# Moving the adaLN tiles, bias tables, two norm weights and the sink logits from SyncE's queue to GpSimd's, with a ring of three

## The reference

```python
# first block, D = 2048
mod = silu(c) @ w_ada + b_ada                  # w_ada is 2048 x 12288
sh1, sc1, ga1, sh2, sc2, ga2 = split(mod, 6)
h = modulate(rms_norm(x, g_norm1), sh1, sc1)
qa, ka, va, oa, gates, qb, kb, vb = split(h @ w_in)
h_a = mlstm_bidirectional(...)                 # 4 heads, then a norm times g_head_a * sigmoid(oa)
h_b = neighborhood_attention(qb, kb, vb, rpb)  # 8 heads, bias from the table rpb
x = x + ga1 * (concat([h_a, h_b]) @ w_out)
h = modulate(rms_norm(x, g_norm2), sh2, sc2)
x = x + ga2 * conv_glu(h, w_up, conv_w, conv_b, w_down)    # 2 x 5632 wide
x = rms_norm(x, g_final)
# second block
q..., ga, gb = split(rms_norm(x, norm_mix_g) @ w_in_2)
ya = sliding_window_attention(..., sink_logits) @ w_branch_a
yb = stick_breaking_attention(...) @ w_branch_b
x = x + (sigmoid(ga) * ya + sigmoid(gb) * yb) @ w_out_2
x = x + swiglu(rms_norm(x, norm_ffn_g), w_ffn_in, w_ffn_down)
return rms_norm(x, norm_final_g)
```

## Time and profile before

| | |
|---|---|
| times of three runs | 2805.21, 2807.12, 2807.06 us |
| median | 2807.06 us |
| the profiled execution, its time | 2805.28 us |
| the profiled execution, its span | 2803.5 us |
| mean granted TensorE clock in it | 0.993 of full |
| PE busy | 2632.0 us, 94% |
| DVE busy | 1647.8 us, 59% |
| ACT busy | 1203.2 us, 43% |
| POOL busy | 132.6 us, 5% |

### The profile page before, as it was taken

The page is one execution under the profiler, slowest core; times in us unless marked ns, Lnnn a source line. Parts: engine busy times, 40 slices in busy tenths (PEclk is TensorE's granted clock), DMA queues, the critical chain, the costliest instruction groups (busy, mean ns, idle before and its releaser), DMA issues.

```text
span 2803.5 us, 33726 instructions
## 1 busy us (share of the span) xinstructions
PE 2632.0 (94%) x11966; PEld 2153.8 (77%) x11966; DVE 1647.8 (59%) x1822; ACT 1203.2 (43%) x1516; POOL 132.6 (5%) x129
## 2 busy tenths in 40 slices
PE   0699998989999999999989999999999999999998
PEld 0577886778878788788878877778788888888886
DVE  8887674767767665644454465555555444454444
ACT  1143344434434343444444454554454454544443
POOL 2000003010000000000010030101000000000000
PEclk9999999999999999999999999999999999999999
DMA  9798776676767665555566644346566666666664
GB/s 397 275 339 276 251 263 168 206 237 197 245 202 240 194 194 165 187 189 192 167 203 191 191 121 143 100 140 219 162 185 188 192 188 188 188 189 191 194 193 147
DMA packets 273259, 567.38 MB, mean 202 GB/s; under 512 B 23956, under 2 KB 24300, under 8 KB 272652
## 3 DMA queue, kind: packets, MB, share of 16 engines
q1 hardware_dynamic: 272528, 565.78, 63.2%
q0 software_dynamic: 208, 0.18, 0.0%
q10 hardware_dynamic: 428, 0.14, 0.0%
HBM read 563.94 MB, written 2.10 MB: 202 GB/s over the span
## 4 chain that ended last, share of the span: by engine, by line
PE 82%; DVE 6%; DMA 5%; issue 3%; ACT 2%; SPq 1%; DVEq 0%; POOL 0%; POOLq 0%; ACTq 0%
PE gp L1127 25%; PE gp L1129 25%; PE gp L1128 25%; DMA raw<-in_w_in_dram 2%; DVE ada_sum L1622 2%; DMA ada_ring<-in_w_ada_dram 2%; DVE w_lo L1519 1%; ACT w_hi L685 1%; DMA proj<-in_w_ada_dram 1%; PE tp L1354 1%; PE tp L1396 1%; PE tp L1172 1%; PE tp L1163 0%; PE tp L1262 0%; DVE ff L1880 0%
## 5 line engine op out<-in xcount | busy, mean ns | idle before, releaser
L1519 DVE TENSOR_TENSOR w_lo<-raw,w_hi 128x1024 fp32r<-128x1024 f32 x872 | 1068.4, 1229 | 903.2 <-ACT w_hi L685 898.3
L685 ACT CAST w_hi<-raw 128x1024 fp32r<-128x1024 f32 x872 | 910.9, 1051 | 1114.8 <-PE gp L1129 896.1
L1127 PE MATMUL gp<-w_hi,h_hi 128*128 128x512 f32 x2656 | 1051.0, 396 | 33.7 <-DVE w_lo L1519 30.0
L1128 PE MATMUL gp<-w_lo,h_hi 128*128 128x512 f32 x2656 | 1036.2, 390 | 0.0
L1129 PE MATMUL gp<-w_hi,h_lo 128*128 128x512 f32 x2656 | 1036.1, 390 | 0.0
L1127 PEld LDWEIGHTS gp<-w_hi,h_hi 128*128 128x128 f32 x2656 | 499.6, 188 | 152.7 <-DVE w_lo L1519 40.9
L1129 PEld LDWEIGHTS gp<-w_hi,h_lo 128*128 128x128 f32 x2656 | 499.4, 188 | 106.1
L1128 PEld LDWEIGHTS gp<-w_lo,h_hi 128*128 128x128 f32 x2656 | 499.8, 188 | 100.7 <-issue 0.2
L1127 PE MATMUL gp<-w_hi,a_hi 128*128 128x512 f32 x704 | 274.7, 390 | 0.0
L1129 PE MATMUL gp<-w_hi,a_lo 128*128 128x512 f32 x704 | 273.9, 389 | 0.0
L1128 PE MATMUL gp<-w_lo,a_hi 128*128 128x512 f32 x704 | 273.9, 389 | 0.0
(11 more groups left out here) (264 smaller groups left out, 1436.0 us busy)
## 6 DMA issues: line engine op xcount, KB each, us to landing
raw<-in_w_in_dram SPq DMA_DIRECT2D x248, 512.0 KB, 4.4
raw<-in_w_up_dram SPq DMA_DIRECT2D x176, 512.0 KB, 4.3
raw<-in_w_ffn_in_dram SPq DMA_DIRECT2D x176, 512.0 KB, 4.2
ada_ring<-in_w_ada_dram SPq DMA_DIRECT2D x128, 512.0 KB, 4.6
raw<-in_w_down_dram SPq DMA_DIRECT2D x88, 512.0 KB, 3.7
raw<-in_w_ffn_down_dram SPq DMA_DIRECT2D x88, 512.0 KB, 4.6
proj<-in_w_ada_dram SPq DMA_DIRECT2D x64, 512.0 KB, 7.5
raw<-in_w_out_dram SPq DMA_DIRECT2D x64, 512.0 KB, 4.6
```

The source lines that it names most:

```text
L685: nc.scalar.copy(w_hi[:, s], raw[:, s]).then_inc(hi_ready, 1)
L1127: mm(o, hi[:, kt0 + kt, ps], w_hi[:, s, k, :], start=n == 0, stop=False)
L1128: mm(o, hi[:, kt0 + kt, ps], w_lo[:, s, k, :], start=False, stop=False)
L1519: V.tensor_tensor(w_lo[:, s], raw[:, s], w_hi[:, s].bitcast(F32), ALU.subtract).then_inc(lo_ready, 1)
```

## The change

All later adaLN tiles, the bias tables, g_final, the sink logits and norm_final_g_2 are issued by GpSimd, in one written-out order between its other work. The ring of adaLN tiles has three slots (AR = 3; the last 32 tiles, from PART3 on, use only two of them). SyncE issues x, the first 64 tiles, the blocks of weights and the output. GpSimd's first later tile stands behind the clearing of the sum buffer at L538 of the changed kernel. In `g_in_o` DVE now sums a tile at each odd block of both chunks, where it summed one at each of the first four. A few small buffers take the place of an unused one, so that the third slot fits.

```diff
+AR = 3
...
-        ada_ring = sb("ada_ring", [P, 2, ADA_W], scope=s1)
+        ada_ring = sb("ada_ring", [P, AR, ADA_W], scope=s1)
...
+        def ada_slot(a):
+            return (a - PART2) % AR if a < PART3 else (a - PART3) % 2
...
@@ SyncE
-            def ada(a, slot, k, col):
-                if not isinstance(a, int) or a >= PART2 + 2:
-                    sp.wait_ge(ada_summed, a - 1)
-                sp.dma_start(ada_ring[:, slot, :], w_ada[bass.ds(k * P, P), bass.ds(col, ADA_W)]
-                             ).then_inc(ada_landed[slot], 16)
...
-            def bias(n):
-                if n < 4:
-                    sp.wait_ge(ml_s, HA)
-                else:
-                    sp.wait_ge(na_s, n - 3)
...
-            stream(g_in_a, ada_in(0), g_in_b)
-            stream(g_in_b, ada_in(g_in_a.chunks), g_in_o)
-            stream(g_in_o, biases, g_out, unrolled=True)
-            stream(g_out, ada_out, g_up)
-            stream(g_up, None, g_down, early=ada_up)
-            stream(g_down, None, g_in2a)
-            sp.wait_ge(drained[1], g_down.chunk0 + g_down.chunks)
-            sp.dma_start(gate2[:, :], ... g_final ...)
-            sp.wait_ge(x_final, 2 * (g_out.chunks + g_down.chunks))
-            sp.dma_start(sink[:, :], ... sink_logits_2 ...)
...
+            for g, nxt in zip(gemms, gemms[1:]):
+                stream(g, nxt)
@@ GpSimd
+            def ada(a, k, col):
+                if a >= PART3 + 2:
+                    pool.wait_ge(ada_summed, a - 1)
+                elif a >= PART3:
+                    pool.wait_ge(ada_summed, PART3)
+                elif a >= PART2 + AR:
+                    pool.wait_ge(ada_summed, a - AR + 1)
+                s = ada_slot(a)
+                pool.dma_start(ada_ring[:, s, :], w_ada[k * P:(k + 1) * P, col:col + ADA_W]
+                               ).then_inc(ada_landed[s], 16)
...
+            for k in range(K1 - 1):
+                ada_cols(k)
+            for n in range(4):
+                bias(n)
+            ada_cols(K1 - 1)
+            for n in range(3):
+                ada_gate(n)
+            for n in range(4):
+                window(n)
+            ada_gate(3)
+            bias(4)
+            ada_gate(4)
+            bias(5)
+            window(4)
...
             pool.wait_ge(na_s, HB)
             link(nc.gpsimd.memset(gate2[:, :], 0.0))
             pool.dma_start(gate2[0:1, :], b_ada[0:1, 5 * D:6 * D]).then_inc(acc_bias[2], 16)
+            ada_mod(0, range(4))
+            ada_mod(1, range(4))
+            ada_mod(2, range(3))
+            add_x(g_out, xt1, 0)
...
+            for c_ in range(g_down.chunks):
+                add_x(g_down, ff, c_)
+            pool.wait_ge(drained[1], g_down.chunk0 + g_down.chunks)
+            pool.dma_start(gate2[:, :], ... g_final ...)
+            pool.dma_start(sink[:, :], ... sink_logits_2 ...)
@@ VectorE, in g_in_o
-                if j < 4:
-                    n = 4 * e + j
-                    dve.wait_ge(ada_landed[n % 2], 16 * (3 * K1 + n // 2 + 1))
+                if j % 2:
+                    n = (e * g_in_o.nb + j) // 2
+                    dve.wait_ge(ada_landed[ada_slot(PART2B + n)], ada_count(PART2B + n))
```

167 lines of the change are left out of this document (80 added, 87 removed).

## The result

The changed kernel takes 2785.23 us (median of four runs, 2783.74 to 2786.3), the kernel before 2807.09 (2805.21 to 2808.13): a ratio of 0.992, with an interval of 0.9908 to 0.9932. The forecast was 2785.0. The sum came out right. But two of its terms, A and D, come from the third slot and not from the queue, and C only in part from the queue; that is what most of this part is about.

What follows compares the result with a forecast made beforehand. The prediction took the kernel to be bound by its matmuls on PE. Terms 5.0 + 1.3 + 13.4 + 1.8 + 1.5 - 0.7 = 22.3 us off 2805.28 gave 2783.0, as a median 2784.8, stated as 2785; range 2777 to 2798.

Steps and rivals of the forecast that it cites:

- A: First projection: SyncE no longer stands in adaLN issues that wait for DVE's sums, so weights run ahead; gain 5.0 us.
- D: `g_out`: weights loaded ahead let DVE's delay beside POOL's addition fall into the ring's slack; gain 1.8 us.
- C: Second projection to `g_in_o`: weights no longer stand behind bias transfers and adaLN tiles on SyncE; gain 13.4 us.
- With SyncE free of them the weights run as far ahead as their ring lets them: First projection: freed of four adaLN issues taking 7.61 us, SyncE issues weights earlier; 5.0 of 5.6 us taken.
- B: Gates of the mLSTM: gate-logit copies no longer stand behind a DVE sum waiting for its tile; gain 1.3 us.
- E: Into the second block: weights come earlier without g_final and the sink logits on SyncE; gain 1.5 us.
- F: Start of `g_up`: 32 tiles still use two slots, and slower landing from POOL lengthens DVE's wait; loss 0.7 us.
- Landings of 9 to 11 us: Rival: POOL's tiles land that late, costing gains in `g_in_a`; 2791 to 2798 us, chance 0.14.
- The slower rival: `g_in_a`: POOL writes descriptors only in DVE's gaps, so landings stretch to 13 to 15 us; 2829 to 2853, chance 0.09.
- The rival of the bias tables: Before `g_in_o`: eight slow bias issues on POOL hold up the last set of six tiles; 2794 us, chance 0.10.

## Why the prediction was right, and where it wasn't

**A, 5.0 forecast, 4.9 to 5.1 measured, and for half of the reason.** The step "With SyncE free of them the weights run as far ahead as their ring lets them" named the queue as the cause. The path was right, since ACT waited 69.6 us for weights from 120 to 240 us of the kernel before. But with SyncE free and two slots the gain is gone (-0.8), and with everything on SyncE and three slots it is whole (5.2). What limited the stretch was the round trip of a slot: wait for the sum, issue, landing, next sum. By the prediction's own formula two slots leave 2 x 2.70 - 1.28 = 4.1 us for issue and landing where tiles stand in adjacent blocks, and they took 0.34 + 4.3 from SyncE and 0.53 + 4.3 from GpSimd; three slots leave 6.8, and the changed kernel took 0.53 + 5.9. SyncE's 7.61 us were that round trip, seen from the engine that stood in it. The prediction did say that the third slot was the cover on which the move to GpSimd rests, and the run with the ring of two bears that out; it failed to ask what the slot does by itself.

**B, 1.3 forecast, 1.0 to 1.1 in its stretch.** DVE's wait in front of the gate copies is gone, as forecast. The ring alone gives 1.3 and the queue alone 0.6, but this column is at -0.7 and -5.5 in kernels that change nothing there, so the runs don't say which of the two it was.

**C, 13.4 forecast, 13.9 in its place and 12.9 to 13.7 with the stretch ahead of it.** Here several things count. The ring alone gives 4.3, sums at odd blocks alone 5.9, the queue with those sums and two slots 13.9 less 4.1 that it loses ahead. With the ring of three, moving only the bias tables gives 12.2, and moving only the tiles, with their sums at odd blocks, 13.6: the stall was the two together, 9.36 us of issues and then a chain of sum, wait and landing behind them, against 10.8 us of weights loaded ahead. How much the move of the tiles adds to ring and odd blocks is not shown, since those two weren't run together on SyncE.

**D, 1.8 forecast, 2.3 measured.** The ring again (2.3 with it alone, -0.2 with the queue alone). I had put it down to POOL's addition beside DVE's sum and to late weights, of which a free queue was to be the cure; the slot was. (Of the two engines slowing each other the row shows one side: DVE's sum at 1.94 us.)

**E, 1.5 forecast, 1.2 to 2.7 by the run that undoes it.** Right as argued: ACT's wait for weights goes with the two transfers and comes back with them. It is the one part that only the queue gives.

**F, -0.7 forecast, -0.8 to -1.0.** DVE's wait for a tile grows as argued (1.14 to 2.00 us), and the version that puts the last 32 tiles back on SyncE gets about half of it back (-0.4 in that stretch; PE's wait is 0.75 us and not 1.30, against 0.42 before).

**The rivals.** Landings of 9 to 11 us did not come (5.8). The slower rival did not come either. Of the rule that GpSimd cannot write descriptors under VectorE's two-port operations (the Trainium skill, SBUF — State Buffer, "SBUF: two separate sides") nothing is seen here: with two slots and DVE busy for 47 of 60 us, tiles land in 4.3 us from GpSimd and in 4.3 from SyncE. The second half of what the Trainium skill states there, that operations with two SBUF inputs don't lock GpSimd out unless it reads, agrees, since DVE's sums and subtractions there have two such inputs. The rival of the bias tables was half right. I put the delay into GpSimd's issues at up to 2.5 us each; they take 0.65 (5.23 us for eight), and the delay is in the transfers, 13.6 us for tiles and weights alike. In the place that the change gives them no sum of DVE waits for a tile and PE never stops. That place matters: behind the set it costs 7.6 us more.

**The range and the chances.** The range held the time with room on both sides. That the sum was within a microsecond is partly luck: the errors of reason in A and D hide behind one edit that made the slot and the queue come together, and by the table the stretches sum to 19.0 and 20.4 us, not to 22.3. The medians differ by 21.9, and the profiled execution of before was 1.8 below its median. The range of 2779 to 2791 that the prediction gives "by the bounds" doesn't follow from them either: its bounds sum to a gain of at most 24.0 us, or 2783, and of at least 1 us, or 2806.

## What to carry to other kernels

When a change moves an issue to another queue and also deepens its ring, price the two apart before adding: a wait that shows up on the issuing engine may be the round trip through too few slots, and then any engine would stand in it. The check is short: (slots x spacing of the consumer) less its own time, against issue and landing. A queue that mixes a stream with waits of another stream needs either to be parted or to have more loaded ahead than the longest of those waits. And a burst of transfers in small pieces belongs where the most is loaded ahead, whichever queue issues it, since it slows everything in flight.
